# Two attentions rebuilt in head pairs, with bias, mask and minimum in one VectorE pass

## The chip, the cores and the metric

The kernel runs on one core of a Trainium2 chip. The metric is the device time of one execution in microseconds. Before the change it is 2356.97 us, the median of three runs (2353.76 to 2362.44). TensorE, VectorE, ScalarE, GpSimd and the DMA queues have their own instruction streams; they meet in semaphores that the kernel sets by hand.

## The reference, cut to what matters

Two transformer blocks on 256 tokens of width 2048, all in float32. The first block has 16 sliding-window heads with a distance bias and a sink ("swa") and 16 heads with a forget gate ("fox"). The second has 16 heads over 256 tokens and 256 context tokens, with a window mask and a sink.

```python
# block 1: swa heads, window 128, 2 key/value heads
s = jnp.einsum('bnqkgd,bnskd->bnkgqs', qb, kb) * scale
s = s - slopes[:, :, None, None] * dist
s = jnp.where(mask[None, :, None, None], s, -jnp.inf)
m = jnp.maximum(jnp.max(s, axis=-1, keepdims=True), sink)
p = jnp.exp(s - m)
p = p / (jnp.sum(p, axis=-1, keepdims=True) + jnp.exp(sink - m))
# block 1: fox heads, cT = cumsum of log f, per head
s = jnp.einsum('bqhd,bshd->bhqs', q_blk, k) * scale
s = s + c_blk[..., None] - cT[:, :, None, :]
s = jnp.where((q_pos[:, None] >= k_pos[None, :])[None, None], s, -jnp.inf)
p = jax.nn.softmax(s, axis=-1)
# block 2: windowed scores, context scores and a sink in one softmax
p = jax.nn.softmax(jnp.concatenate([s_win, s_ctx, s_sink], axis=-1), axis=-1)
# block 2 also needs silu(c) @ w_ada, in six parts of 2048 columns
m = jax.nn.silu(cond) @ w + b
```

Around the attentions stand large matrix products: in, out, up, down in the first block, in, out and an MLP in the second.

## The kernel before

**Large products.** A weight matrix comes in chunks of 512 columns. A chunk is 8 steps (6 in the last down part), a step 256 rows of the weight. For each step ScalarE rounds the weight to `w_hi` (`hi`, L526), VectorE makes the rest `w_lo` (`lo`, L811), and TensorE does 12 products of 512 columns (L1308 to L1310). `body` on each engine walks a chunk, three steps ahead of TensorE; four slots hold the split weights. The stages are in1, out1, up1a, down1a, up1b, down1b, up1c, down1c, in2, out2 and mlp2.

**The adaptive part.** GpSimd loads tiles of `w_ada` (L395), and VectorE adds each, times a column of silu, to an accumulator (`ada_op`, L826; L923 in in1), between its `lo` instructions. A part that serves tokens and context has two accumulators, so two VectorE instructions per tile. `ADA_ORDER` names the parts and their accumulators, `ADA_RUNS` cuts them into runs (part index, first tile, count). Run 1 (16 tiles, one accumulator) runs during attention 1, run 2 in out1, runs 3 to 6 in up1a, down1a, up1b and down1b; run 6 has two accumulators, up1c has none. After a part TensorE sums over partitions (`ada_sum`, L1353, 16 products of one column for each accumulator) and VectorE clears the accumulators (`ada_clear`, L848).

**Attention 1.** Heads 0 to 15 are swa, 16 to 31 fox. `qk1` holds the queries and keys turned, two heads in one tile of 128 rows: an even head has rows 0 to 63, an odd one rows 64 to 127. For one head `scores1` puts the bias into one of four PSUM banks of G by a product (L1413: `slope_id`, an identity times the head's slope made by ScalarE at L575, with the table of distances; for fox L1417 with `cT` and two mask products, L1419), then adds the score products of both query blocks (L1421: 128 and 256 columns, 64 rows deep). VectorE takes two maxima (L998, L999), scales and negates them (`shift`), ScalarE takes two exponentials out of PSUM with the row sums as accumulator output (L600, L602), TensorE turns the result (L1430), ScalarE copies it out of PSUM (L617), TensorE multiplies by the values (L1440 to L1443, 64 columns each), and every four heads VectorE divides (L985 to L987). All float32 products are two records each in the trace.

**Attention 2.** The same loop over 32 units of one head and one query block: scores of 512 columns (L1563), a mask product (L1565), maximum (L1206), exponential (L736), four transposes, copy (L749), four products by the values (L1577).

**What sets the order.** Each engine runs its list in program order. `attend` on TensorE issues three scores ahead, then for head n: scores of n+3, transposes of n, values of n-2.

## Time and profile before

| | |
|---|---|
| median of 3 runs | 2356.97 us |
| the profiled execution, its own time | 2354.01 us |
| its span, first to last instruction | 2352.3 us |
| TensorE busy | 96% of the span |
| VectorE busy | 65% |
| ScalarE busy | 46% |
| mean granted TensorE clock | 0.973 |

The profile is one execution. A row of a time line has the start in us from the start of the span, the duration, the engine and line, the operation, what it writes and reads, the shape, and how many instructions are merged (x4). Durations of TensorE records overlap, because their ends are modelled: how long a product holds the engine is read from start to start. A row with [idle before <-releaser] names what ended the engine's idle time.

### The profile page before, as it was taken

To read this page: it belongs to the slowest core of one execution; us is meant where nothing else is said; L and a number is where in the kernel's file an instruction comes from. 1 tells how busy PE (TensorE), PEld (TensorE's weight loads), DVE (VectorE), ACT (ScalarE), POOL (GpSimd) and SP (SyncE) were. 2 spreads that over 40 slices of the span, in tenths; PEclk is the share of its full clock that TensorE was granted. 3 is DMA by queue.
4 is the path that set the end of the run, shared out by engine and by line. 5 is a ranking of instruction groups with operands and counts; after the bars stand their busy time and mean duration, and the time that the engine had idled before them with its cause. 6 is when DMAs were issued, how large, how long until landed. Compare 5 with 4: busy or idle time off the path is not lost.

```text
span 2352.3 us, 30732 instructions
## 1 busy us (share of the span) xinstructions
PE 2251.9 (96%) x10407; PEld 1847.5 (79%) x10407; DVE 1538.2 (65%) x1750; ACT 1082.0 (46%) x1487; POOL 122.3 (5%) x217
## 2 busy tenths in 40 slices
PE   7999989899999999999997999898999999999997
PEld 5888678688888888788876776786888888888876
DVE  6886657778897888946665363455655655655555
ACT  5444554455534555335546344345444443443433
POOL 1000000100100000000000000001000000000000
PEclk9998999899999999989998999999999999999999
DMA  7886228678889787856554350155666666666752
GB/s 265 289 289 211 81 81 290 210 252 279 281 270 288 258 288 255 270 170 202 191 179 147 115 177 3 63 188 196 220 210 215 215 214 209 221 205 210 229 166 102
DMA packets 267279, 482.53 MB, mean 205 GB/s; under 512 B 15180, under 2 KB 107604, under 8 KB 265888
## 3 DMA queue, kind: packets, MB, share of 16 engines
q1 hardware_dynamic: 236544, 367.18, 47.1%
q0 software_dynamic: 29808, 113.63, 15.4%
q8 instruction: 81, 1.33, 0.2%
q10 hardware_dynamic: 816, 0.15, 0.0%
q14 instruction: 30, 0.25, 0.0%
HBM read 478.79 MB, written 2.11 MB: 204 GB/s over the span
## 4 chain that ended last, share of the span: by engine, by line
PE 94%; ACT 3%; DVE 2%; issue 1%; DMA 1%; ACTq 0%; SPq 0%; DVEq 0%
PE G L1308 27%; PE G L1310 27%; PE G L1309 27%; PE G L1563 1%; PE T L1353 1%; PE T L1477 1%; PE T L1430 1%; PE G L1421 1%; PE T L1577 1%; PE T L1342 1%; ACT junk L476 1%; PE G L1565 1%; PE G L1413 0%; PE G L1417 0%; DMA raw<-in_w_in 0%
## 5 line engine op out<-in xcount | busy, mean ns | idle before, releaser
L811 DVE TENSOR_TENSOR w_lo<-raw,w_hi 128x1024 fp32r<-128x1024 f32 x696 | 844.6, 1223 | 520.3 <-ACT w_hi L526 516.0
L526 ACT ACTIVATE w_hi<-raw 128x1024 fp32r<-128x1024 f32 x696 | 736.1, 1060 | 934.0 <-PE G L1310 932.5
L1308 PE MATMUL G<-w_hi,h_hi 128*128 128x512 f32 (+1 forms) x1920 | 755.3, 393 | 14.0 <-ACT w_hi L526 7.6
L1309 PE MATMUL G<-w_lo,h_hi 128*128 128x512 f32 (+1 forms) x1920 | 750.3, 391 | 0.0
L1310 PE MATMUL G<-w_hi,h_lo 128*128 128x512 f32 (+1 forms) x1920 | 749.9, 391 | 0.0
L1308 PEld LDWEIGHTS G<-w_hi,h_hi 128*128 128x128 f32 x1920 | 365.2, 190 | 89.8 <-ACT w_hi L526 8.6
L1310 PEld LDWEIGHTS G<-w_hi,h_lo 128*128 128x128 f32 x1920 | 364.7, 190 | 75.4
L1309 PEld LDWEIGHTS G<-w_lo,h_hi 128*128 128x128 f32 x1920 | 365.1, 190 | 73.5
L1308 PE MATMUL G<-w_hi,a_hi 128*128 128x512 f32 x896 | 352.6, 393 | 5.0 <-issue 2.9
L1310 PE MATMUL G<-w_hi,a_lo 128*128 128x512 f32 x896 | 349.9, 391 | 0.0
L1309 PE MATMUL G<-w_lo,a_hi 128*128 128x512 f32 x896 | 349.8, 390 | 0.0
L826 DVE SCALAR_TENSOR_TENSOR ada_acc<-ada_w,silu,ada_acc 128x1024 f32<-128x1024 f32 x160 | 204.9, 1280 | 61.4 <-DMA ada_w<-in_w_ada 60.8
L1308 PEld LDWEIGHTS G<-w_hi,a_hi 128*128 128x128 f32 x896 | 168.9, 189 | 44.1 <-issue 7.2
L1310 PEld LDWEIGHTS G<-w_hi,a_lo 128*128 128x128 f32 x896 | 168.9, 188 | 35.6
L1309 PEld LDWEIGHTS G<-w_lo,a_hi 128*128 128x128 f32 x896 | 169.1, 189 | 35.2 <-issue 0.5
L395 POOL DMA_DIRECT2D ada_w<-in_w_ada x192 | 101.7, 530 | 1417.8 <-DVE ada_acc L826 1082.0
L923 DVE SCALAR_TENSOR_TENSOR ada_acc<-ada_w,silu,ada_acc 128x1024 f32<-128x1024 f32 x64 | 79.2, 1279 | 0.0
L1068 DVE SCALAR_TENSOR_TENSOR conv<-T,convw,conv 128x255 f32<-128x255 f32 (+1 forms) x176 | 72.7, 475 | 9.4 <-ACT conv L659 7.0
L1206 DVE TENSOR_REDUCE mx<-G 128x1 f32<-128x512 f32 x32 | 22.1, 692 | 47.3 <-PE G L1565 47.3
L1342 PE MATMUL T<-ident,y 128*128 128x128 f32 x96 | 18.0, 358 | 32.0 <-ACT y L487 24.9
L1091 DVE TENSOR_TENSOR y<-y,G 128x512 f32<-128x512 f32 x56 | 35.9, 683 | 16.0 <-PE G L1310 16.0
L549 ACT ACTIVATE u_buf<-G,rstdx 128x512 f32<-128x512 f32 x44 | 27.9, 686 | 36.1 <-PE G L1310 36.1
(215 smaller groups left out, 1338.6 us busy)
## 6 DMA issues: line engine op xcount, KB each, us to landing
ada_w<-in_w_ada POOLq DMA_DIRECT2D x192, 512.0 KB, 4.9
raw<-in_w_up SPq DMA_DIRECT2D x176, 512.0 KB, 5.7
raw<-in_w_mlp_up SPq DMA_DIRECT2D x128, 512.0 KB, 4.6
raw<-in_w_mlp_down SPq DMA_DIRECT2D x128, 512.0 KB, 4.8
raw<-in_w_in SPq DMA_DIRECT2D x104, 512.0 KB, 5.2
raw<-in_w_down SPq DMA_DIRECT2D x88, 512.0 KB, 5.6
raw<-in_w_out SPq DMA_DIRECT2D x64, 512.0 KB, 5.0
raw<-in_w_in SPq DMA_DIRECT2D x8, 272.0 KB, 4.2
```

Of the source, the lines that this page charges most:

```text
L395: pool.dma_start(ada_tiles(run)[:, half, :], w_ada[:, bass.ds(t + first // 2, 1), part * D + half * ADA_HALF:part * D + (half + 1) * ADA_HALF]
L526: act.activation(w_hi[:, s % 4], raw[:, s // 2 % 4, STEPK * (s % 2):STEPK * (s % 2) + STEPK, :], ACT.Copy).then_inc(hi_ready, 1)
L549: act.activation(dst(b), G[:, 2 * parity + b, 0:width], func, scale=scale).then_inc(bank_evac, 1)
L811: dve.tensor_tensor(w_lo[:, s % 4], raw[:, s // 2 % 4, STEPK * (s % 2):STEPK * (s % 2) + STEPK, :], w_hi[:, s % 4].bitcast(F32), ALU.subtr ...
L826: ins = dve.scalar_tensor_tensor(out=acc[:, half, :], in0=ada_tiles(run)[:, half, :], scalar=silu[:, c, bass.ds(dt + (first + k) // 2, 1)] ...
L923: ins = dve.scalar_tensor_tensor(out=ada_acc[:, c, half, :], in0=ada_w[:, half, :], scalar=silu[:, c, bass.ds(i * 2 + k // 4, 1)], in1=ada ...
L1068: ins = dve.scalar_tensor_tensor(out=conv[:, j, k:TOK], in0=tt(0)[:, j, 0:TOK - k], scalar=convw[:, tap, bass.ds(t + dt, 1)], in1=conv[:, ...
L1091: dve.tensor_tensor(y[:, b, c * N:c * N + N], y[:, b, c * N:c * N + N], G[:, 2 * (c % 2) + b, :], ALU.add).then_inc(bank_evac, 1)
L1308: pe.matmul(out, ah, wh, start=f, stop=False)
L1309: pe.matmul(out, ah, wl, start=False, stop=False)
L1310: mm = pe.matmul(out, al, wh, start=False, stop=l)
L1342: mm = pe.transpose(tt(g % 2)[:, j, b * P:b * P + P], src[:, b, (4 * g + j) * P:(4 * g + j + 1) * P], ident[:])
```

## The change

It rebuilds both attentions and moves the adaptive part's runs.

- The bias of the swa heads no longer comes from a product. Queries are scaled by scale/slope as they are copied out of PSUM (`qscale`), and VectorE does one pass out of PSUM (`tensor_tensor_reduce`): score plus table, times minus the slope (or minus the scale), written to SBUF, with the minimum against the negated sink as accumulator output. In the fox heads and in attention 2 the masks are in this pass too; the fox heads keep one bias product of 384 columns, now in the rounded format of the large products (`select`, `cT`), for which `cT` is split into a rounded part and its rest, in rows 0 to 15 and 32 to 47.
- `exps1` and `exps2` read SBUF and have no accumulator output. The row sum comes from a column of ones beside the values (`vx1`, `vx2`, 65 columns), filled by GpSimd and ScalarE.
- The unit of the loops is a pair of heads. The scores of a pair go out one head at a time: both blocks of the even head, then both of the odd one. TensorE's order is: transposes of pair j, scores of pair j+2, values of pair j-1. In attention 1 ScalarE copies the turned even head and VectorE the odd one. VectorE divides after every pair.
- The slope copies (L575) are gone. No adaptive tile is taken during attention 1: out1 has run 1 with two accumulators, up1c gets 16 tiles with one accumulator, and down1b has one accumulator in place of two. The first tile of a run is written by a product alone, so the clears are gone. The sum that was in up1a is in down1a, the double sum moves from up1c to up1b, and down1c gets one.

```diff
-ADA_RUNS = ((0, 0, 32), (1, 0, 16), (1, 16, 16), (2, 0, 32), (4, 0, 16), (3, 0, 32), (4, 16, 16), (5, 0, 32))
+ADA_ORDER = ((0, (0, 1)), (3, (2,)), (1, (0, 1)), (4, (2,)), (2, (0,)), (5, (0,)))
...
+ADA_RUNS = ((0, 0, 32), (2, 0, 16), (1, 0, 32), (2, 16, 16), (3, 0, 32), (4, 0, 16), (4, 16, 16), (5, 0, 32))
...
+    t[:, C_QS:C_QS + 8] = SCALE / SLOPES[2 * np.arange(8)[None, :] + p // DH]
...
+    vx1 = place("vx1", [P, NB, 18, PV], "tmp")
...
-        for h in range(HEADS):
-            act.activation(slope_id[:, h, :], ident[:], ACT.Copy, scale=float(slopes[h] / SCALE)).then_inc(slope_ready, 1)
...
+            ins.then_inc(qk_act, 1)
+        act.wait_ge(v_ones, 1)
+        for b in range(NB):
+            ins = act.activation(vx1[:, b, 0:2, 0:DH], p1[:, b, VA:VA + 2 * DH].rearrange("p (h d) -> p h d", d=DH), ACT.Copy)
+        ins.then_inc(va_ready, 1)
+
+        def exps1(j):
+
+            for i in range(2):
+                n = 2 * j + i
+                act.wait_ge(masked, n + 1)
+                act.activation(sm1[:, n % 4, 0:P], sm1[:, n % 4, 0:P], ACT.Exp, scale=-1.0,
+                               bias=nm[:, j % 4, 2 * i:2 * i + 1])
+                act.activation(sm1[:, n % 4, P:3 * P], sm1[:, n % 4, P:3 * P], ACT.Exp, scale=-1.0,
+                               bias=nm[:, j % 4, 2 * i + 1:2 * i + 2]).then_inc(p_ready, 1)
+            if j < 8:
+                act.wait_ge(es_in, j + 1)
+                act.activation(es[:, j % 4, :], es[:, j % 4, :], ACT.Exp).then_inc(es_ready, 1)
...
+                if first + k < 2 and run != ADA_LAST:
+                    ins = dve.tensor_scalar(acc[:, half, :], ada_w[:, half, :], silu[:, c, 0:1], None, ALU.mult)
+                else:
+                    ins = dve.scalar_tensor_tensor(out=acc[:, half, :], in0=ada_tiles(run)[:, half, :],
+                                                   scalar=silu[:, c, bass.ds(dt + (first + k) // 2, 1)],
+                                                   in1=acc[:, half, :], op0=ALU.mult, op1=ALU.add)
             ins.then_inc(ada_used, 1)
...
 
...
+            else:
+                ins = dve.tensor_copy(qk1[:, 4 * g + 2:4 * g + 4, :], tt(g % 2)[:, 2:4, :])
+            ins.then_inc(qk_dve, 1)
...
+        for c0, n in ((0, P), (P, TOK)):
+            ins = dve.tensor_scalar(cT[0:48, c0:c0 + n], G[0:48, 1, 0:n], -1 / SCALE, None, ALU.mult)
+        link(ins)
+        for c0, n in ((0, P), (P, TOK)):
+            ins = dve.scalar_tensor_tensor(out=cT[32:48, c0:c0 + n], in0=G[32:48, 1, 0:n], scalar=-1 / SCALE,
+                                           in1=cT[32:48, c0:c0 + n].bitcast(F32), op0=ALU.mult, op1=ALU.subtract)
+        ins.then_inc(c_ready, 1)
         for g in range(2, 6):
             turned1(g)
...
-        def shift(n, slot, cols, nsinks):
...
+        def masks1(j):
+
+            dve.wait_ge(s_ready, j + 1)
+            for i in range(2):
+                n = 2 * j + i
+                if j >= 2:
+                    dve.wait_ge(pt_turned, n - 3)
+                table, scale, limit = ((ALI, -float(SLOPES[n]), nsink[:, 0, n:n + 1]) if n < HEADS else (CAU, -SCALE, BIG))
+                for k, (c0, w) in enumerate(((0, P), (P, 2 * P))):
+                    ins = dve.tensor_tensor_reduce(out=sm1[:, n % 4, c0:c0 + w], in0=G[:, n % 4, c0:c0 + w],
+                                                   in1=tab1[:, table + c0:table + c0 + w], scale=scale, scalar=limit,
+                                                   op0=ALU.add, op1=ALU.min,
+                                                   accum_out=nm[:, j % 4, 2 * i + k:2 * i + k + 1])
+                ins.then_inc(masked, 1)
             if exped is not None:
                 dve.wait_ge(es_ready, exped)
-                link(dve.tensor_tensor(r, r, es[:, b % 4, :], ALU.add))
-            link(dve.reciprocal(r, r))
-            dve.tensor_tensor(dst.rearrange("p k (h d) -> p k h d", d=DH),
-                              T[:, 2 + b % 2, :].rearrange("p (k h d) -> p k h d", k=NB, d=DH),
...
+            dve.tensor_tensor(dst.rearrange("p k (i d) -> p k i d", d=DH),
...
+        for j in range(HEADS):
+            dve.wait_ge(pt_turned, 2 * j + 2)
+            if j >= 2:
+                dve.wait_ge(pt_used, 2 * j - 2)
+            dve.tensor_copy(pt1[:, (2 * j + 1) % 4, :], T[:, 1, 0:3 * P]).then_inc(pt_dve, 1)
+            if j + 2 < HEADS:
+                masks1(j + 2)
+            if j >= 1:
+                outputs1(j - 1)
...
                 if k % 2:
-                    ada_op(2, 4 * c + k // 2)
...
-        for g, n, run_up, run_down, fin_up, fin_down in (("a", 8, 3, 4, None, 2), ("b", 8, 5, 6, None, 3),
-                                                         ("c", 6, None, None, 4, None)):
+        for g, n, run_up, run_down, fin_up, fin_down in (("a", 8, 2, 3, None, 1), ("b", 8, 4, 5, 2, 3),
+                                                         ("c", 6, 6, None, None, 4)):
...
+            first, each = (4, 4) if n == 8 else (1, 3)
+            body(s0, adas=[(run_up, k) for k in range(first)])
...
-        def scores1(n):
-
...
-            if n >= 4:
-                pe.wait_ge(p_ready, n - 3)
-            if n < HEADS:
-                pe.matmul(bank[:, 0:3 * P], slope_id[:, h, :], tab1[:, ALI:ALI + 3 * P], start=True, stop=False)
-            else:
-
-
-                pe.matmul(bank[:, 0:3 * P], ident[:, h:h + 1].broadcast_to([P, P]), cT[:], start=True, stop=False)
-                for c0 in (0, 2 * P):
-                    pe.matmul(bank[:, c0:c0 + P], ident[:], tab1[:, CAU:CAU + P], start=False, stop=False)
-            for blk, (c0, w) in enumerate(((0, P), (P, 2 * P))):
-                mm = pe.matmul(bank[:, c0:c0 + w], qk1[rows, q, P * blk:P * blk + P], qk1[rows, k, 0:w],
-                               start=False, stop=blk == NB - 1)
+        def scores1(j):
+
+            if j >= 2:
+                pe.wait_ge(masked, 2 * j - 2)
+            if j >= 8:
+                for n in (2 * j, 2 * j + 1):
+                    h = n - HEADS
+                    pe.matmul(G[:, n % 4, 0:3 * P], select[:, h:h + 1].broadcast_to([P, P]), cT[:], start=True, stop=False)
+            for i in range(2):
+                for blk, (c0, w) in enumerate(((0, P), (P, 2 * P))):
+                    n = 2 * j + i
+                    h = n % HEADS
+                    q, k = (h // 2, 8 + h // 8) if n < HEADS else (10 + h // 2, 18 + h // 2)
+                    rows = slice(DH * i, DH * i + DH)
+                    mm = pe.matmul(G[:, n % 4, c0:c0 + w], qk1[rows, q, P * blk:P * blk + P], qk1[rows, k, 0:w],
+                                   start=j < 8, stop=j < 8 or blk == NB - 1)
             mm.then_inc(s_ready, 1)
...
+                v = n // 8 if n < HEADS else 2 + n - HEADS
+                out = T[:, 2 + j % 2, 2 * PV * i:2 * PV * i + 2 * PV]
+                pe.matmul(out[:, 0:PV], pt1[:, n % 4, 0:P], vx1[:, 0, v, :], start=True, stop=True)
+                pe.matmul(out[:, PV:2 * PV], pt1[:, n % 4, P:2 * P], vx1[:, 0, v, :], start=True, stop=False)
+                pe.matmul(out[:, PV:2 * PV], pt1[:, n % 4, 2 * P:3 * P], vx1[:, 1, v, :],
+                          start=False, stop=True).then_inc(pt_used, 1)
...
+            scores(0)
+            scores(1)
+            for j in range(HEADS):
+                turn(j)
+                if j + 2 < HEADS:
+                    scores(j + 2)
+                if j >= 1:
+                    pv(j - 1)
+            pv(HEADS - 1)
...
-                ada_sum(1)
...
+        def scores2(j):
+            t, blk = j // 2, j % 2
+            if j >= 2:
+                pe.wait_ge(masked, 32 + 2 * j - 2)
+            if j == 1:
```

`masks2`, `exps2`, `pv2` and `turn2` are built as in attention 1, with 512 columns for a head and block.

How the order of instructions changes. First TensorE in the swa heads of attention 1, in a steady stretch, before (one head):

```order
L1413 MATMUL G<-tab_74,slope_id 128x384
L1421 MATMUL G<-qk_73 128x128
L1421 MATMUL G<-qk_73 128x256
L1430 MATMUL T<-ident,sm_69 128x128 x3
L1440 MATMUL T<-p_68,pt_70 128x64
L1441 MATMUL T<-p_68,pt_70 128x64
L1443 MATMUL T<-p_68,pt_70 128x64
```

and now, TensorE at the same place (two heads; `vx_71` are the values with their ones):

```order
L1478 MATMUL T<-consts,sm_69 128x128 x6
L1471 MATMUL G<-qk_73 128x128
L1471 MATMUL G<-qk_73 128x256
L1471 MATMUL G<-qk_73 128x128
L1471 MATMUL G<-qk_73 128x256
L1501 MATMUL T<-vx_71,pt_70 128x65
L1502 MATMUL T<-vx_71,pt_70 128x65
```

The bias product of each head is gone, and the four score products of a pair stand together; four more value products follow the last row.

VectorE in the same stretch, before (two heads, with one adaptive tile):

```order
L998 TENSOR_REDUCE mx<-G 128x1
L999 TENSOR_REDUCE mx<-G 128x1
L971 TENSOR_SCALAR nm<-mx,nsink 128x2
L998 TENSOR_REDUCE mx<-G 128x1
L999 TENSOR_REDUCE mx<-G 128x1
L971 TENSOR_SCALAR nm<-mx,nsink 128x2
L976 TENSOR_TENSOR es<-nm,sink_110 128x8
L826 SCALAR_TENSOR_TENSOR ada_acc<-ada_w,silu,ada_acc 128x1024
```

and now, VectorE for one pair (ISA is the fused pass, the row with nm alone the reading of its accumulator):

```order
L1048 COPY pt_70<-T 128x384
L1031 ISA sm_69,nm<-G,tab_74,nsink 128x128
L1031 ISA nm 128x1
L1031 ISA sm_69,nm<-G,tab_74,nsink 128x256
L1031 ISA nm 128x1
L1031 ISA sm_69,nm<-G,tab_74,nsink 128x128
L1031 ISA nm 128x1
L1031 ISA sm_69,nm<-G,tab_74,nsink 128x256
L1031 ISA nm 128x1
L1002 TENSOR_TENSOR es<-nm,sink_111 128x4
L1013 TENSOR_TENSOR rs<-T,es 128x4
L1014 RECIPROCAL rs<-rs 128x4
```

Maxima and adaptive tile make room for the fused passes, a copy and a division for each pair (its product, 128x2x128, follows the last row).

VectorE in the second chunk of down1b, before, and then now:

```order
L848 MEMSET ada_acc 128x2048
L811 TENSOR_TENSOR w_lo<-raw,w_hi 128x1024
L826 SCALAR_TENSOR_TENSOR ada_acc<-ada_w,silu,ada_acc 128x1024
L826 SCALAR_TENSOR_TENSOR ada_third<-ada_w,silu,ada_third 128x1024
L811 TENSOR_TENSOR w_lo<-raw,w_hi 128x1024
```

Here it is in the changed kernel, VectorE again:

```order
L870 MEMSET ones_again 128x1
L837 TENSOR_TENSOR w_lo<-raw,w_hi 128x1024
L855 SCALAR_TENSOR_TENSOR ada_acc<-ada_w,silu,ada_acc 128x1024
L837 TENSOR_TENSOR w_lo<-raw,w_hi 128x1024
L855 SCALAR_TENSOR_TENSOR ada_acc<-ada_w,silu,ada_acc 128x1024
```

Between two `w_lo` stands one adaptive instruction in place of two, and the clear is gone.

## Rows read from the trace of the kernel before

**Rows 1.** The page: busy us (share of the span) and instructions by engine.

```profile
PE 2251.9 (96%) x10407; PEld 1847.5 (79%) x10407; DVE 1538.2 (65%) x1750; ACT 1082.0 (46%) x1487; POOL 122.3 (5%) x217
```

**Rows 2.** Windows (swa heads, in2, attention 2): us, busy PE, PEld, DVE, ACT, POOL; clock.

```profile
242.00:278.00 36.00, 36.00 (x188) 22.45 (x188) 26.83 (x62) 19.75 (x75) 3.69 (x7) 1.00 0.31 90
...
1330.00:1350.00 20.00, 20.00 (x90) 16.57 (x89) 3.68 (x3) 4.14 (x4) 0.00 (x0) 1.00 0.32 98
1403.00:1491.00 88.00, 88.00 (x513) 61.28 (x514) 32.83 (x77) 44.94 (x103) 1.42 (x2) 1.00 0.09 32
```

**Rows 3.** Time line of TensorE: one swa head, bias to bias.

```profile
256.20 0.86 PE L1413 MATMUL G<-tab,slope_id 128*128 128x384 f32 x2
256.99 0.92 PE L1421 MATMUL G<-qk 64*128 64x128 f32 x4
257.84 0.55 PE L1430 MATMUL T<-ident,sm 128*128 128x128 f32 x3
258.23 0.33 PE L1440 MATMUL T<-p,pt 128*128 128x64 f32 x2
...
258.84 0.54 PE L1413 MATMUL G<-tab,slope_id 128*128 128x384 f32 x1
```

**Rows 4.** Time line of TensorE: bias and masks of one fox head.

```profile
292.36 0.86 PE L1417 MATMUL G<-cT,ident 128*128 128x384 f32 x2
293.06 0.61 PE L1419 MATMUL G<-tab,ident 128*128 128x128 f32 x4
293.60 0.37 PE L1421 MATMUL G<-qk 64*128 64x128 f32 x1
```

**Rows 5.** Time line of TensorE: one unit of attention 2.

```profile
1438.57 1.12 PE L1563 MATMUL G<-k2t,q2t 64*128 64x512 f32 x2
1439.62 0.49 PE L1565 MATMUL G<-tab,ident 128*128 128x128 f32 x2
1439.94 0.60 PE L1430 MATMUL T<-ident,sm 128*128 128x128 f32 x4
1440.38 0.56 PE L1577 MATMUL T<-p,pt 128*128 128x64 f32 x4
...
1441.32 0.69 PE L1563 MATMUL G<-k2t,q2t 64*128 64x512 f32 x1
```

**Rows 6.** Time line of VectorE, then of ScalarE, in the swa heads.

```profile
257.95 0.29 DVE L998 TENSOR_REDUCE mx<-G 128x1 f32<-128x128 f32 x1 [1.76 <-PE G L1421]
258.15 0.41 DVE L999 TENSOR_REDUCE mx<-G 128x1 f32<-128x256 f32 x1
...
258.43 0.49 ACT L617 ACTIVATE pt<-T 128x384 f32<-128x384 f32 x1 [1.29 <-PE T L1430]
258.87 0.37 ACT L600 ACTIVATE sm<-G,nm 128x128 f32<-128x128 f32 x1
259.13 0.19 ACT L600 ACTIVATION_READ_ACCUMULATOR sm<-G,nm 128x1 f32 x1
```

**Rows 7.** Time line of ScalarE: the slope copies at the end of in1.

```profile
204.96 3.30 ACT L575 ACTIVATE slope_id<-ident 128x128 f32<-128x128 f32 x16
```

**Rows 8.** TensorE's waits, 200 to 215 us: total, times, longest.

```profile
PE G L1308 <- ACT w_hi L526: 2.4, 1, 2.4
```

**Rows 9.** Time line of VectorE before attention 1: the making of cT.

```profile
236.81 0.38 DVE L957 MEMSET cT<- 128x384 f32 x1 [0.27 <-PE G L1389]
...
237.43 0.40 DVE L959 TENSOR_SCALAR cT<-G 16x256 f32<-16x256 f32 x1
```

**Rows 10.** Time line of VectorE, second chunk of down1b: two neighbouring w_lo.

```profile
951.83 1.22 DVE L811 TENSOR_TENSOR w_lo<-raw,w_hi 128x1024 fp32r<-128x1024 f32 x1
...
955.36 1.22 DVE L811 TENSOR_TENSOR w_lo<-raw,w_hi 128x1024 fp32r<-128x1024 f32 x1
```

**Rows 11.** TensorE's waits, 915 to 1020 us (down1b).

```profile
PE G L1308 <- issue: 2.1, 4, 0.6
PE G L1308 <- ACT w_hi L526: 1.6, 2, 1.2
```

381 lines of the change are left out of this document (188 added, 193 removed).

## The prediction

> **What bounds the kernel now.** I read the page's busy table first: TensorE is busy for 96% of the span, VectorE for 65%, ScalarE for 46% [rows 1]. Then the windows of the two attentions: in the swa heads and in attention 2 TensorE is busy without a break at a granted clock of 1.00, while VectorE is busy for 75% and 37% and ScalarE for 55% and 51% [rows 2]. So both attentions last as long as TensorE's list, and what leaves that list is gained, as long as nobody else becomes the last. The third view is TensorE's own time line, read from start to start [rows 3 to 5]; it gives the prices. The fourth is TensorE's waits in the stages whose side work moves [rows 8, 11].
>
> **Attention 1, TensorE.** A swa head takes 258.84 - 256.20 = 2.64 us: bias 0.79, scores 0.85, transposes 0.39, values 0.61 [rows 3]. A fox head has the same parts, but its bias takes 0.70, because no product of another height follows it, and its masks 0.54 [rows 4]: 2.64 - 0.09 + 0.54 = 3.09. Sixteen of each make 91.7 us. The 0.09 is a wait as TensorE goes over to products 64 rows deep. In the score products themselves there is more of this kind: the bias sends 384 columns through twice in 0.70, and the scores, which are the same 384 columns twice, need 0.85.
>
> A swa pair then costs: 0.09 for going over, 0.85 for the first head's scores, at most 0.70 for the second's (the bias row, same columns, no change of height between them; 0.64 if its first weight load is hidden), 2 x 0.39 for the transposes, 2 x 0.61 for the values. That is 3.64; with the lower prices 3.5; I take 3.6, where two heads took 5.29. The 65th column is no new instruction, and the value products are paced by something other than their columns (0.61 for six records of 64, 0.39 for three of 128), so it costs nothing. A fox pair adds two products of 384 columns in the rounded format. Steady in2 has 88 to 90 such products of 512 columns in 20 us, 0.227 each [rows 2]; 384 columns are 0.17 by columns and 0.227 at most. With 0.17 a fox pair takes 3.95 against 6.18. Eight pairs of each: 28.8 + 31.6 = 60.4.
>
> The start is new: no value products fill it. Scores of pair 0 take 1.6, VectorE's pass over its two heads about 1.7, two exponentials each 0.4 to 0.5, and ScalarE has the exponentials of pair 1 in front of the copy of pair 0, which pair 1's transposes wait for. Laid out by hand, TensorE idles some 0.5 before the transposes of pair 0's second head and 1.0 before those of pair 1: +1.5 (0 to 3). **Attention 1: 91.7 to 61.9, -29.8.**
>
> **Does VectorE follow?** Its list for a swa pair: four fused passes, four accumulator reads, one copy of 384 columns, the sink's addition, and add, reciprocal and product of the division. The trace before has no fused pass. Its nearest rows are the maxima out of PSUM, 0.29 for 128 and 0.41 for 256 columns, the second starting 0.20 after the first [rows 6]. The nearest row for an accumulator read is ScalarE's, 0.19 [rows 6]. Low end: passes 0.20 + 0.33 and reads of 0.06 each, 1.3 a pair; high end: 0.29 + 0.41 and reads of 0.19, 2.2. I take 1.8, nearer to neither, because starts overlap in those rows but the reads must wait for the pass. The copy is about 0.5 (ScalarE's of the same size 0.49 [rows 6]), the sink 0.2, the division about 0.85 with its two links. Sum 3.35, from 2.85 to 3.75, against TensorE's 3.6. In fox pairs sink and addition are gone: 2.9 against 3.95. ScalarE: four exponentials of 0.37 to 0.47, a copy of 0.49, a sink of 0.2, 2.4 in all; the accumulator reads are off its list. The chain from the scores of a pair to its transposes two pairs later is scores 1.6, passes 1.8, last exponentials 0.9, transposes 0.8 and some 0.3 of signals, 5.4 for two pairs, against 7.2. So TensorE stays last, with VectorE close behind.
>
> **Attention 2.** A unit takes 2.75: scores 1.05, mask 0.32, transposes 0.44, values 0.94 with the going over [rows 5]. A pair after the change: 0.10, 1.05, 0.85 for the second head (1.05 less the weight load at its start and the wait at its end, 0.1 each), 2 x 0.44, 2 x 0.90: 4.7 against 5.49. Start 0.6. VectorE needs about 1.8 for two passes of 512, ScalarE 2.7; both have room. 32 x 2.75 = 88.0 becomes 75.8, **-12.2** (-11 to -13). ScalarE's four copies of values and GpSimd's fill before it stand in in2, where `w_hi` is three steps ahead: nothing, or 1 if that lead is used up.
>
> **Around attention 1.** The slope copies hold ScalarE for 3.30 [rows 7], and TensorE waits 2.4 for the `w_hi` behind them [rows 8]: **-2.4**. Before the scores VectorE gets more to do: `cT` had a clear of 0.38 and two scalings of up to 0.40 [rows 9]; two more passes of that kind, one for `select`, one more subtraction, and each of the first two copies of queries in halves. That is about 1.6, of which 0.5 fits in VectorE's waits; the rest delays the copies that the scores wait for: **+1.1** (0 to 2). The last division is of 256 columns in place of 512: -0.3. GpSimd's fill and copies of values lie between its last in1 tile and out1's row, where it only waits.
>
> **The adaptive part.** VectorE pays 3.53 for a `w_lo` and two adaptive instructions [rows 10], so 1.17 and two of 1.18; TensorE's step is 12 x 0.227 = 2.72. In down1b four steps running have two of them, and TensorE waited 2.1 + 1.6 = 3.7 [rows 11]; the clear goes too. With one accumulator a step costs VectorE 2.35 and nothing is late: **-5** (-3.7 to -7, the smaller pauses included). Out1 takes over the two accumulators, but alternates them with `w_lo`: 8 x 1.17 + 8 x 1.18 + two evictions of 0.68 is 20.2 a chunk against 21.8 for TensorE. It fits, and the last eviction may come later: **+0.5** (0 to 3). Up1b gets the double sum while VectorE also has four tiles a chunk: **+1** (0 to 3). Up1c has room for three. The sums themselves are as many as before: 0.
>
> **Sum.** -29.8 - 12.2 - 2.4 + 1.1 - 0.3 - 5 + 0.5 + 1 = -47.1. The profiled execution took 2354.0, so 2306.9. The median of the runs lies 3.0 above that execution, within their spread of 8.7; I leave it there: 2307.
>
> **Rivals.**
>
> *The two heads' scores overlap.* The even head uses rows 0 to 63, the odd one 64 to 127, in different banks, and now they follow each other directly. No row shows two such neighbours, so neither for nor against, but the waits at the change of height speak for a separate mode. One head at a time, only the last pass of the even head and the first of the odd one can meet: 0.43 a pair in attention 2 (a pass of 512, half of 0.85), 0.21 in attention 1. 16 x 0.64 = 10.2: 2297. The Trainium skill, "TensorE: Matmul & The Clock Gate", Part 3 on row and column tiling, says that matmuls in different row groups run concurrently, starting some 4 ns apart. By that rule the time is this rival's, without it the forecast's; no run here shows it yet.
>
> *VectorE becomes the last in the swa pairs.* At its high end, 3.75 to 3.9, it adds 8 x 0.3 = 2.4. If the fused pass takes twice as long per column, 768 columns add 0.8 a pair: 4.4 for swa, level with fox: 8 x 0.8 = +6, with late first pairs up to +10: 2313 to 2317. The rows speak against doubling, as two-input passes of 1024 columns take 1.2 [rows 10]. The Trainium skill, "Vector Engine (DVE) Microarchitecture Reference", section 7, warns that such an operation with two SBUF sources of full width runs at half throughput for want of a port for the accumulator. Here one source is in PSUM, and the pass of 1024 columns with two SBUF sources, in 1.22 [rows 10], is not halved; taken for the fused pass, the warning would give this rival's time.
>
> *The adaptive work bites where it went.* If out1, up1b and down1a each wait as down1b did (3.7 to 7), +15: 2322. For it: out1's margin is 1.6 a chunk. Against: its tiles are spread, not four in a row.
>
> *Slower than before.* The fused pass is an instruction that no row shows. Were it slow per column, VectorE would set both attentions. At c us per column, 16 pairs of 768 and 16 of 1024 columns, plus about 50 for the rest of its list, reach 180 us and the 5 gained elsewhere at c = 0.0048. From 4.8 ns per column the kernel is slower than before; at 6 ns by 35 us, 2389. Every VectorE row here is near 1.2 ns. That the rebuilding changes nothing would need VectorE at exactly that point.
>
> **Chances.** Forecast 0.43; overlap 0.28; VectorE last 0.14; adaptive work 0.10; slower 0.02; within 0.5% 0.03. The range goes from the overlap with the lower prices of a pair (2297 less 8) to the adaptive rival: 2289 to 2322. About 0.5%, 12 us, is what a measurement can tell from no change. Faster 0.95, same 0.03, slower 0.02.
>
> **What would show it.** In the time line of TensorE: a swa pair of 3.6 and a fox pair of 3.95, from one group of six transposes to the next, and a unit pair of 4.7 in attention 2; with overlap 3.4, 3.75 and 4.3, and two score products of different heads starting almost together. No wait of TensorE for VectorE or ScalarE inside the attentions after pair 1. Fused passes of 0.3 and 0.45 with reads of 0.06 to 0.19. VectorE busy for some 90% of the swa stretch. No ScalarE wait at the end of in1, no waits in down1b, and out1 at 21.8 a chunk. The prediction is wrong if TensorE waits in every pair, if the granted clock in the attentions falls from 1.00 to its lower level (1.2 GHz), or if out1 or up1b grow by more than 3 each.

## The result and the profile after

The changed kernel takes 2284.29 us (median of 4 runs, 2280.0 to 2287.6), the kernel before beside it 2356.76 us. The ratio is 0.9689, 95% interval 0.9676 to 0.9701: faster by 72.5 us. The prediction said faster, with 2307 us in a range from 2289 to 2322: the sign was right, the time lies 5 us below the range. The profiled execution of the changed kernel took 2284.72 us against 2354.01, 69.3 us less where 47.1 were forecast.

The busy line of its page stands where [rows 1] stood:

```profile
PE 2182.4 (96%) x10231; PEld 1807.9 (79%) x10231; DVE 1526.3 (67%) x1841; ACT 1066.9 (47%) x1375; POOL 125.7 (6%) x220
```

The shares hardly moved. The windows of the two attentions (swa pairs, fox pairs, attention 2), which answer to [rows 2], have the granted clock at 1.00 throughout. TensorE is idle for 1.7 of the first 20 us and for 1.1 of the 63, both at the start of an attention; behind it (244 to 290 and 1366 to 1421 us) the view of its waits is empty:

```profile
core 0: us, PE busy (x) PEld busy (x) DVE busy (x) ACT busy (x) POOL busy (x), PEclk, DMA share, GB/s
238.00:258.00 20.00, 18.29 (x158) 14.54 (x158) 17.58 (x86) 14.97 (x45) 0.00 (x0) 1.00 0.01 1
258.00:290.00 32.00, 32.00 (x274) 27.35 (x273) 22.69 (x105) 21.15 (x59) 0.00 (x0) 1.00 0.01 2
1358.00:1421.00 63.00, 61.89 (x449) 46.95 (x450) 29.44 (x93) 42.20 (x75) 1.42 (x2) 1.00 0.12 44
```

So after its first pairs each attention is still as long as TensorE's list, and the list must be shorter than I made it. Its time line over a swa pair and the next transposes answers to [rows 3] (start, duration, engine, line, operation, shape, how many merged):

```profile
249.30 0.83 PE L1478 MATMUL T<-consts,sm 128*128 128x128 f32 x6
250.06 0.93 PE L1471 MATMUL G<-qk 64*128 64x128 f32 x8
250.92 0.44 PE L1501 MATMUL T<-vx,pt 128*128 128x65 f32 x2
251.19 0.39 PE L1502 MATMUL T<-vx,pt 128*128 128x65 f32 x2
251.42 0.39 PE L1503 MATMUL T<-vx,pt 128*128 128x65 f32 x2
251.64 0.39 PE L1501 MATMUL T<-vx,pt 128*128 128x65 f32 x2
251.86 0.39 PE L1502 MATMUL T<-vx,pt 128*128 128x65 f32 x2
252.09 0.39 PE L1503 MATMUL T<-vx,pt 128*128 128x65 f32 x2
252.31 0.50 PE L1478 MATMUL T<-consts,sm 128*128 128x128 f32 x3
```

From 249.30 to 252.31 a pair takes 3.01 us, not 3.6. Transposes take 0.76 (priced 0.78) and values 1.39 (priced 1.22: each product now takes 0.22 or more, also the one that took 0.16 with 64 columns). The scores are far off: eight records, both heads, start at 250.06 and what follows starts at 250.92, 0.86 us, the 0.85 of one head's four records in [rows 3]. Attention 2 shows the same, against [rows 5]:

```profile
1379.22 0.93 PE L1478 MATMUL T<-consts,sm 128*128 128x128 f32 x7
1380.08 1.13 PE L1626 MATMUL G<-k2t,q2t 64*128 64x512 f32 x4
1381.13 2.00 PE L1646 MATMUL T<-vx,pt 128*128 128x65 f32 x16
```

Two heads' scores of 512 columns in 1.05 us, which is what one head takes. Taken singly, the eight records of the swa pair start at 250.059, .073, .274, .286, .385, .398, .604 and .616: in couples, 12 to 14 ns apart, the first couple with 128 columns each, as the second, the last two with 256. In attention 2 they are 7 ns apart. The program has 128, 128, 256 and 256 columns of the even head first and the same of the odd head after them, so the starts do not follow the program. A record does not name its head; that a couple is the same pass of both heads is the reading that fits, and the experiments test it.

Where the 69.3 us lie, from the two traces (TensorE's first and last record of each stretch, the bias products of the kernel before counted with the scores; the third column is a second profile of the same changed kernel, from the experiments, and its change stands in brackets):

| stretch | before | after | again | change, forecast |
|---|---|---|---|---|
| start to first score of attention 1 | 241.8 | 237.9 | 238.5 | -3.9 (-3.3), -1.3 |
| attention 1 | 92.3 | 52.7 | 52.7 | -39.5, -29.8 |
| from there to the first score of attention 2 | 1068.8 | 1067.2 | 1069.8 | -1.5 (+1.1), -3.8 |
| attention 2, to its last value product | 88.1 | 63.2 | 63.2 | -24.9, -12.2 |
| the rest | 861.3 | 861.9 | 859.8 | +0.6 (-1.5), 0 |

The two attentions alone are 22.4 us better than forecast, which is the whole error. The stretch between the attentions takes 1063.9 to 1073.1 us in eight profiles with the same work there, and the last stretch 859.7 to 863.0, so single stages in them are read with care.

### The profile page after: what moved, and what is told of

The parts are those of the page before. It is cut to its first block, busy times and chain, and to the rows that moved or that the text cites. A ratio compares the mean times of both kernels' runs of the same rounds, so it can differ in the third digit from the quotient of the medians.

```text
span 2283.0 us, 30329 instructions
## 1 busy us (share of the span) xinstructions
PE 2182.4 (96%) x10231; PEld 1807.9 (79%) x10231; DVE 1526.3 (67%) x1841; ACT 1066.9 (47%) x1375; POOL 125.7 (6%) x220
## 4 chain that ended last, share of the span: by engine, by line
PE 93%; ACT 3%; DVE 2%; DMA 1%; issue 1%; ACTq 0%; SPq 0%; DVEq 0%; POOLq 0%; POOL 0%
PE G L1362 28%; PE G L1364 28%; PE G L1363 28%; PE T L1407 1%; PE T L1537 1%; PE T L1646 1%; PE T L1396 1%; PE T L1478 1%; ACT junk L491 1%; PE G L1626 1%; DMA x<-in_x 1%; PE G L1471 1%; PE T L1501 0%; DMA raw<-in_w_in 0%; PE T L1451 0%
## 5 line engine op out<-in xcount | busy, mean ns | idle before, releaser
L1364 PEld LDWEIGHTS G<-w_hi,h_lo 128*128 128x128 f32 x1920 | 363.3, 189 | 75.3
L855 DVE SCALAR_TENSOR_TENSOR ada_acc<-ada_w,silu,ada_acc 128x1024 f32<-128x1024 f32 x122 | 153.6, 1279 | 31.7 <-DMA ada_w<-in_w_ada 31.7
L855 DVE SCALAR_TENSOR_TENSOR ada_third<-ada_w,silu,ada_third 128x1024 f32<-128x1024 f32 x60 | 76.9, 1281 | 56.3 <-DMA ada_w<-in_w_ada 56.3
L945 DVE SCALAR_TENSOR_TENSOR ada_acc<-ada_w,silu,ada_acc 128x1024 f32<-128x1024 f32 x64 | 79.2, 1279 | 0.0
L1396 PE MATMUL T<-consts,y 128*128 128x128 f32 x96 | 19.1, 374 | 31.0 <-ACT y L502 24.2
```

What stands on the lines that cost most here:

```text
L855: ins = dve.scalar_tensor_tensor(out=acc[:, half, :], in0=ada_tiles(run)[:, half, :], scalar=silu[:, c, bass.ds(dt + (first + k) // 2, 1)] ...
L945: ins = dve.scalar_tensor_tensor(out=ada_acc[:, c, half, :], in0=ada_w[:, half, :], scalar=silu[:, c, bass.ds(i * 2 + k // 4, 1)], in1=ada ...
L1364: mm = pe.matmul(out, al, wh, start=False, stop=l)
L1396: mm = pe.transpose(tt(g % 2)[:, j, b * P:b * P + P], src[:, b, (4 * g + j) * P:(4 * g + j + 1) * P], ident)
```

## The experiments

The theory after the result: **the products of the two heads use different halves of TensorE's rows and run side by side from the first pass to the last, whatever their order in the program; the forecast's only large error is the price of the second head's scores.** The rivals were that the order matters, and that the pair is short for another reason: VectorE, or a cheaper change of height (going between products 128 and 64 rows deep).

**Both heads on the same rows.** Nothing but the rows of the operands changes, in both attentions.

```diff
-                    rows = slice(DH * i, DH * i + DH)
+                    rows = slice(0, DH)
```

> The changed kernel with the score products of both heads of a pair on partitions 0 to 63, in both attentions: the odd head's scores are worked out from the even head's rows of the queries and keys, so the odd heads' outputs are those of other scores; number, size and order of all instructions stay. Theory 'the whole error of the forecast is the second head's scores, which ran beside the first's': its price comes back, 16 x 0.59 in attention 1 (swa pair 3.01 to 3.60, fox pair 3.36 to 3.95) and 16 x 0.83 in attention 2 (unit pair 3.87 to 4.70), 22.7 us in all: 2307 us (2302 to 2310), which is what the forecast gave. Rival 'the pair is short for another reason, such as cheaper passes between row groups, and VectorE sets 3.01 in the swa pairs': under 8 us more, 2292 us or less.

Measured: 2304.0 us, ratio to before 0.977 (0.9749 to 0.9791), 20 us more than the changed kernel. Its time line of TensorE:

```profile
249.76 1.03 PE L1471 MATMUL G<-qk 64*128 64x256 f32 x5
250.72 0.44 PE L1501 MATMUL T<-vx,pt 128*128 128x65 f32 x2
...
252.11 0.82 PE L1478 MATMUL T<-consts,sm 128*128 128x128 f32 x6
252.87 1.57 PE L1471 MATMUL G<-qk 64*128 64x128 f32 x8
254.37 0.32 PE L1501 MATMUL T<-vx,pt 128*128 128x65 f32 x1
```

The same eight records now take 254.37 - 252.87 = 1.50 us. The swa pair is 3.65, the fox pair 4.00, the unit pair (one pair of heads in attention 2, 3.87 in the changed kernel) 4.72; attention 1 takes 61.7 us and attention 2 75.3. The forecast had 3.6, 3.95, 4.7, 61.9 and 75.8. This is the kernel that I had predicted, and the rival with at most 8 us more is out.

**Alternate order.** In attention 1 the loop over blocks goes outside, the one over heads inside.

```diff
-            for i in range(2):
-                for blk, (c0, w) in enumerate(((0, P), (P, 2 * P))):
+            for blk, (c0, w) in enumerate(((0, P), (P, 2 * P))):
+                for i in range(2):
```

> The changed kernel with attention 1's score products of a pair issued alternately (first block of the even head, first block of the odd head, second block of the even, second of the odd) and not one head at a time. Theory 'the halves run free': the changed kernel's trace shows the eight records of a pair in couples 0.012 to 0.014 us apart although the even head's products all stand first, so order does not matter; 2284 us (2281 to 2287), swa pair 3.01 us, fox pair 3.36, starts in couples as before. Rival 'only neighbours overlap' (the forecast's rival A): alternate order would overlap more than one head at a time; the pair would shorten by up to 0.4 us, 16 times, 2278 us or less.

Measured: 2286.41 us, 0.9705 (0.9686 to 0.9724); pairs of 3.00, 3.35 and 3.87 us, attention 1 52.6 us. The scores of a swa pair take 0.86 us as before:

```profile
250.02 0.93 PE L1471 MATMUL G<-qk 64*128 64x128 f32 x8
250.88 0.44 PE L1501 MATMUL T<-vx,pt 128*128 128x65 f32 x2
```

The couples are now 6 to 7 ns apart in place of 12 to 14, and that is all that the order changes: 0.01 us a pair. "Only neighbours overlap", the limit that I had set in the rival of the overlap, falls.

**A product of all rows between the heads.**

```diff
             for i in range(2):
+                if i and j < 8:
+                    pe.matmul(G[:, (2 * j + 1) % 4, 384:392], ident, ident[:, 0:8], start=True, stop=True)
...
+                if i:
+                    pe.matmul(G[:, (2 * j + 1) % 4, 0:8], ident, ident[:, 0:8], start=True, stop=True)
```

> The changed kernel with one more small product (128 rows, 8 columns) between the even and the odd head's scores, in the 8 swa pairs of attention 1 and the 16 units of attention 2; no result is changed. Theory 'the halves run free of each other only as long as no product that uses all 128 rows stands between them': the overlap is gone there, and the small product comes on top (0.2 to 0.4 us each): swa pair 3.01 to between 3.7 and 4.0, unit pair 3.87 to between 4.8 and 5.1, fox pair 3.36 as before: 2284 + 8 x 0.85 + 16 x 1.1 = 2309 us (2303 to 2315). Rival 'overlap in the records is an artefact and the scores' cost is small for another reason': only the small products are paid, 24 x 0.2 = 5 us, 2289 us.

Measured: 2316.18 us, 0.9824 (0.9808 to 0.9841). TensorE in a swa pair:

```profile
249.81 0.83 PE L1480 MATMUL T<-consts,sm 128*128 128x128 f32 x6
250.57 0.92 PE L1473 MATMUL G<-qk 64*128 64x128 f32 x4
251.42 0.39 PE L1467 MATMUL G<-consts 128*128 128x8 f32 x2
251.74 0.92 PE L1473 MATMUL G<-qk 64*128 64x128 f32 x4
252.59 0.44 PE L1503 MATMUL T<-vx,pt 128*128 128x65 f32 x2
```

A product of 8 columns costs its own 0.32 us (251.42 to 251.74) and parts the heads: 0.85 for each. The swa pair goes to 4.16, a little above the expected 3.7 to 4.0, the unit pair to 5.23, also above; the fox pair, without the product, stays at 3.36. The attentions account for 7.4 + 19.8 = 27.2 of the 32 us; the rest is in the large products between them, where no edit was made, and I have no cause for it beyond their spread.

**The adaptive plan alone**, in the kernel before: its `ADA_ORDER` and `ADA_RUNS`, first tiles by a product, no clears, nothing in attention 1, sums as in the changed kernel.

```diff
-ADA_ORDER = ((0, (0, 1)), (2, (0,)), (3, (0,)), (4, (0,)), (1, (1, 2)), (5, (0,)))
+ADA_ORDER = ((0, (0, 1)), (3, (2,)), (1, (0, 1)), (4, (2,)), (2, (0,)), (5, (0,)))
...
-            if n % 2:
-                ada_op(1, n // 2)
```

> The kernel before, with the changed kernel's plan of the adaptive matrices alone (order of the sums, runs per stage, first tiles multiplied instead of cleared and added, none in attention 1, two accumulators in out1), attentions as before. By the stages of the changed kernel's trace: out1 +4.0, up1a -4.7, down1a +2.0, up1b and up1c 0 together, down1b -6.8, down1c +5.3: -0.2 us, 2356.5 us (2353 to 2359), so the rebuilt attentions and what stands between carry all of the gain. Rival, the forecast's terms for these steps (down1b -5, out1 +0.5, up1b +1, about -3.5, the sum in up1a moved at no net cost): 2353 us, and then out1's +4.0 has another cause than the adaptive work.

Measured: 2351.13 us, median of 10 runs, 0.9973 (0.996 to 0.9986): 3.3 to 9.4 us less than before. My expectation, read off one pair of profiles, had 2356.5 (-0.2) and missed; the forecast's -3.5 is inside the interval. Attention 1 is 92.26 us in both, to the hundredth: VectorE's adaptive tiles there had cost nothing. Of the profiled difference of 5.5 us 2.7 lie ahead of attention 1, where this edit changes nothing; the clock there, shown with the slope copies below, differs between the two profiles. One pair of profiles says no more about the gain than the interval of the runs.

**The slope copies back.**

```diff
+        for h in range(HEADS):
+            act.activation(ada_third[:].rearrange("p a n -> p (a n)")[:, P * h:P * h + P], ident, ACT.Copy, scale=1.0).then_inc(qk_junk, 1)
         body(s0 + 64)
```

> The changed kernel with 16 copies of 128x128 on ScalarE put back ahead of in1's last 8 tiles, where the kernel before made its slope matrices (they write an unused place). Theory: they hold ScalarE's w_hi back by 3.3 us, TensorE waits 2.4 us, in1's last chunk goes from 21.24 to about 24.4 us: +3 us, 2287 us (2286 to 2289). Rival 'ScalarE has that much slack now': the last chunk stays at 21.2 us and nothing is paid, 2284 us; the earlier start of attention 1 would then come from the clock in in1's tail alone.

> The changed kernel once more, so that the three small edits beside it have it on the same chip: 2284 us (2281 to 2287). By the theory that out1's last chunk of 46.7 us in the first profile of it was chance (44.8 in three variants that leave out1 alone, 44.3 in the kernel before), that chunk is 44.8 us here.

Measured, on one chip: 2287.57 us (0.9695, 0.9676 to 0.9714) with the copies, 2283.24 us (0.9671, 0.9651 to 0.969) without. TensorE's waits over the tail of in1 show the old wait, as in [rows 8]:

```profile
PE G L1365 <- ACT w_hi L542: 2.4, 1, 2.4
```

In the profiles 2.0 us arrive at the first score (240.47 against 238.52). The windows of the tail say what the copies cost and what they seem to give back, first with the copies, then without:

```profile
211.20:214.60 3.40, 3.40 (x17) 3.40 (x16) 3.16 (x4) 1.72 (x2) 0.00 (x0) 0.50 0.83 269
219.90:224.80 4.90, 4.90 (x47) 4.90 (x45) 1.28 (x3) 2.67 (x5) 2.55 (x3) 1.00 1.00 338
224.80:229.00 4.20, 4.20 (x21) 4.20 (x21) 0.00 (x0) 0.00 (x0) 0.00 (x0) 0.50 0.22 87
```

```profile
209.00:216.00 7.00, 7.00 (x60) 7.00 (x59) 5.96 (x6) 4.86 (x6) 0.00 (x0) 1.00 0.95 308
219.00:226.80 7.80, 7.80 (x39) 7.80 (x38) 0.00 (x0) 0.00 (x0) 0.60 (x1) 0.50 0.48 187
```

With the copies the clock is at 0.50 for 3.4 us soon after the wait; the kernel before has the same at 212.1. Without the wait it stays at 1.00. From the last product of 512 columns to the adaptive sum, TensorE takes 12.65 us in all ten profiles without the copies, 16.8 in this one and in that of the kernel before, and 15.3 in the adaptive plan alone, which has the copies and the wait but no low clock behind it. So the copies cost 2.6 us there, and 4.1 when the clock falls after the wait.

The adaptive sum behind it is 64 products of one column, and the clock falls a second time within it, in every profile: 2.4 us after its first product in the changed kernel (215.4 and 217.8), 4.9 with the copies (219.9 and 224.8). TensorE was busy without a pause until then; before the sum it ran products of 272 columns and a few transposes at 1.00. A one-column product takes 0.213 us at 0.50 and 0.11 at 1.00, so the sum lasts 8.9 us in the profile with the copies and 10.7 in the one beside it (11.2 in the first of the changed kernel, 11.3 before): 1.8 us by chance for the copies. The removal is worth 2.0 us in this pair of profiles and 4.3 in the medians, whose intervals overlap; the forecast had 2.4, the wait alone.

The second run also speaks on out1's last chunk: 45.8 us in this profile, where 44.8 was expected, 44.8 in three variants, 46.7 in the first, 44.3 before. It varies.

**More work for VectorE in attention 1**: the 256-column pass of each head twice.

```diff
+                ins = dve.tensor_tensor_reduce(out=ada_w[:, 0, 256 * (n % 4):256 * (n % 4) + w], in0=G[:, n % 4, c0:c0 + w],
+                                               in1=tab1[:, table + c0:table + c0 + w], scale=scale, scalar=limit,
+                                               op0=ALU.add, op1=ALU.min,
+                                               accum_out=nmx[:, n % 4:n % 4 + 1])
```

> The changed kernel with the 128x256 pass of every head in attention 1 made twice (the second to an unused place): 2 x (0.48 + 0.08) less the overlap of neighbours, some 1.0 us more for VectorE in each pair. VectorE is busy 17.58 of 20 us in swa pairs (2.65 of 3.01) and 22.69 of 32 in the later pairs (2.39 of 3.36). Theory 'TensorE sets the pairs, VectorE has the slack that its idle time shows': swa pair 3.65 us, fox pair 3.4, +0.64 x 8 + 0.05 x 8 = +5.5 us, 2290 us (2288 to 2292). Rival (the forecast's second rival, VectorE in a closed round with TensorE and ScalarE already at 3.01): every added us is paid, swa pair 4.0, fox pair up to 4.3: +8 to +15 us, 2292 to 2299 us.

Measured: 2289.28 us, 0.9706 (0.9674 to 0.9738), 5 to 6 us more. VectorE's time line (its pair runs from one copy to the next, 3.57 us, without idle time):

```profile
253.68 0.55 DVE L1053 COPY pt<-T 128x384 f32<-128x384 f32 x1
254.15 0.34 DVE L1032 CUSTOM_DVE_ANT_0 sm<-G,tab,nsink 128x128 f32<-128x128 f32 x1
254.41 0.08 DVE L1032 DVE_READ_ACCUMULATOR2_ANT nm<- 128x1 f32 x1
254.41 0.48 DVE L1032 CUSTOM_DVE_ANT_0 sm<-G,tab,nsink 128x256 f32<-128x256 f32 x1
254.82 0.08 DVE L1032 DVE_READ_ACCUMULATOR2_ANT nm<- 128x1 f32 x1
254.82 0.48 DVE L1036 CUSTOM_DVE_ANT_0 ada_w<-G,tab,nsink 128x256 f32<-128x256 f32 x1
255.22 0.08 DVE L1036 DVE_READ_ACCUMULATOR2_ANT nmx<- 128x1 f32 x1
255.22 0.35 DVE L1032 CUSTOM_DVE_ANT_0 sm<-G,tab,nsink 128x128 f32<-128x128 f32 x1
...
257.25 0.55 DVE L1053 COPY pt<-T 128x384 f32<-128x384 f32 x1
```

The added pass takes 0.40 us from start to start, so 0.80 a pair; the list without it is 3.57 - 0.80 = 2.77 us against TensorE's 3.01. VectorE has a slack of 0.24 us in a swa pair, no more. The rival, a closed round in which every added microsecond is paid, would have given 3.81 at this price, and doesn't exist. The fox pairs are back at 3.36 after two longer ones at the change from swa (4.33 and 3.40).

**A bias product back** ahead of each swa head's scores.

```diff
+            if j < 8:
+                for n in (2 * j, 2 * j + 1):
+                    pe.matmul(G[:, n % 4, 0:3 * P], ident, tab1[:, CAU:CAU + 3 * P], start=True, stop=False)
```

> The changed kernel with a product of 128 rows and 384 columns, two passes, ahead of each swa head's scores (identity times the causal mask, added once more, which alters no probability), where the kernel before had its bias product. Theory 'TensorE sets the pairs': each costs what the row of the kernel before shows, 0.79 to 0.85 us, 16 times: swa pair 3.01 to 4.6 or 4.7, fox pair 3.36 as before: +13 us, 2298 us (2296 to 2300). Rival 'VectorE sets the swa pairs' : half of it or less is paid, 2291 us or less.

Measured: 2292.25 us, 0.9723 (0.9699 to 0.9747), 8 to 9 us more. In the steady pairs every added microsecond is paid, so TensorE is last; but the product costs less than expected, and the total, short of the expected 2296 to 2300, alone would not decide against the rival's 2291:

```profile
250.88 1.46 PE L1463 MATMUL G<-tab,consts 128*128 128x384 f32 x4
252.27 0.93 PE L1474 MATMUL G<-qk 64*128 64x128 f32 x8
```

Two take 252.27 - 250.88 = 1.39 us with the 0.09 for going over to 64 rows, and the pair grows from 3.01 to 4.30: 0.64 each, where the row of before had 0.79 in every head. Sixteen of them are 10.3 us; the first pairs, where TensorE had idle time, hide the rest of it. Before, each head went over and back once; a pair does it once, with or without the bias.

**Towards a faster kernel.** Three edits around out1 and the preparations (the two transposed copies of an activation, rounded and rest, that each stage begins with).

```diff
+            elif mid is not None:
+                tile(0, 0, n - 1)
+                tile(0, 1, n)
+                mid()
...
-                if k % 2:
-                    ada_op(1, 4 * c + k // 2)
+                if 8 * c + k in OUT1_AT:
+                    ada_op(1, OUT1_AT.index(8 * c + k))
...
+                if 1 <= t <= n:
+                    scale(t - 1)
+                if pre and t == 2 and n > 3:
+                    pre(3)
+                if t >= 2:
+                    rest(t - 2)
```

`mid` issues x's reload; `OUT1_AT` is 1, 3, 4, 6, 8, 10, 12, 13, 15, 17, 19, 20, 22, 24, 26, 27.

> The changed kernel with three edits around out1: the reload of x is issued after the first two adaptive tiles of out1 instead of after all sixteen (it landed at 398.2 us, 1.9 us after the residual could begin); out1's adaptive work ends three w_lo earlier, so that the last two evictions do not stand behind it (2.0 us late in the profiled execution); and in VectorE's part of each preparation the last group's residual or scaling is put before the first group's h_lo, which waits 2.4 us for ScalarE. Theory 'the chain between out1 and up1 is VectorE's order': up to 2.0 + 1.9 + 3 us there and about 1 us in each of the other preparations: 2277 us (2273 to 2281). Rival 'ScalarE's squares and h_hi set the preparations': 1 to 3 us, 2282 us.

> The changed kernel with the two edits in out1 alone: x's reload after the first two adaptive tiles, and the adaptive work ending three w_lo earlier. Theory 'the last evictions and the reload stand behind the adaptive work': out1's last chunk 44.8 to 42.9 us or less, 2282 us (2280 to 2284). Rival 'all of the gain of the three edits comes from the order in the preparations': 2284 us, as the changed kernel.

> The changed kernel with one edit: in VectorE's part of each preparation the last group's residual or scaling stands before the first group's h_lo. Theory 'each preparation ends 1 to 3 us earlier': 2279 us (2276 to 2282), the last chunks of out1 and down1c and the chunks that hold the two preparations of in2 shorter by that. Rival 'ScalarE's squares and h_hi set the preparations': 2283 us or more.

Measured: all three 2276.14 us, 0.9651 (0.9629 to 0.9673). The two in out1 alone 2286.13 us, 0.9687 (0.9668 to 0.9706), nothing against 2283.24 on the same chip. The order in the preparations alone 2277.39 us, 0.965 (0.9631 to 0.9669), 5.8 us less than the changed kernel beside it. VectorE after out1, first in the changed kernel (its second profile), then with the edit:

```profile
403.57 0.87 DVE L904 TENSOR_SCALAR conv<-T,gains 128x256 f32<-128x256 f32 x2
406.87 1.23 DVE L913 TENSOR_TENSOR h_lo<-u_buf,h_hi 128x1024 fp32r<-128x1024 f32 x1 [2.43 <-ACT h_hi L531]
408.01 1.41 DVE L1080 SCALAR_TENSOR_TENSOR x<-y,rstd,x 128x512 f32<-128x512 f32 x2
```

```profile
400.47 0.88 DVE L904 TENSOR_SCALAR conv<-T,gains 128x256 f32<-128x256 f32 x2
401.26 1.40 DVE L1091 SCALAR_TENSOR_TENSOR x<-y,rstd,x 128x512 f32<-128x512 f32 x2
403.80 1.23 DVE L913 TENSOR_TENSOR h_lo<-u_buf,h_hi 128x1024 fp32r<-128x1024 f32 x1 [1.13 <-ACT h_hi L531]
```

Before the edit VectorE idles 2.43 us for `h_hi` with the last residual ready behind it, for which TensorE's last transposes wait. With it that residual runs at 401.26, inside the wait, of which 1.13 us are left. From out1's first `w_hi` to that of up1a it is 103.7 us against 110.3, and 107.7 to 111.2 in the profiles that leave out1 and this order alone. Part of that is the clock: from 395 to 425 us its mean is 0.89 against 0.77. With the version of all three edits, level with it, it is the fastest of the study. Its difference to the changed kernel, 0.965 against 0.9671, is within the two intervals; the runs themselves (2274.2 to 2278.1 against 2278.8 to 2285.8, five each) don't overlap.

## Why the prediction was wrong, point by point

- **The view and the bound were right.** Attentions as long as TensorE's list, clock 1.00, VectorE close behind in swa pairs, no wait inside after the first pairs. VectorE's margin (2.77 of 3.01 us; estimated 3.35 of 3.6) came out right by luck: its list and TensorE's were both taken 0.6 too long.
- **The step that failed: "at most 0.70 for the second's" in the swa and fox pair, and 0.85 for the second head in attention 2.** Both are 0.01 or less. With the same rows for both heads they are 0.64 and 0.85, and the pairs are 3.65, 4.00 and 4.72 us, attentions 61.7 and 75.3 us, against 61.9 and 75.8 forecast. The term is mis-sized by 9.0 + 12.1 = 21.1 us between these two kernels (attention 1 61.7 against 52.7, attention 2 75.3 against 63.2).
- **Why I took it.** The first rival named the overlap and was given 0.28, but cut to one pass a pair (10.2 us, 2297) by an assumption that no row bore: that a product waits in the program's order for the one before it, even on other rows. The couples in an order that is not the program's, and the alternate order at 2286 us, show that a product on one half does not wait for those ahead of it on the other. The rival with the forecast's full prices, 16 x (0.70 + 0.85) = 24.8 us, would have given 2282. The Trainium skill, "TensorE: Matmul & The Clock Gate", Part 3, says that products in different row groups run concurrently some 4 ns apart: they do run together here, but 6 to 14 ns apart. The same part calls products strictly first in, first out; taken over the whole engine, that was my limit, and here it doesn't hold between the halves. I should have let the range reach to the full overlap: 8 us below 2282, it would have ended near 2274.
- **Start of attention 1**: +1.5 forecast. From the first score to the second group of transposes it takes 2.64 + 2.71 us, with 0.96 us idle before the first group and 0.61 before the second; the next pair takes 3.06, and then the steady 3.01 begins. Right in kind and size. Attention 1 with the same rows is 61.7 against 61.9.
- **The parts of a pair.** 3.65 against 3.6 is in part luck. With the same rows, transposes and going over are 0.76 (priced 0.87), scores 1.50 (1.55), values 1.39 (1.22): the values cost 0.17 more than forecast, the rest less.
- **Bias**: its row had 0.79, its product alone is worth 0.64. The sum was unaffected, since I had built the pair from the parts that stay and not by subtraction.
- **Fused pass**: 0.35 and 0.48 us for 128 and 256 columns, reads 0.08, 0.75 for 512 columns; forecast 0.3, 0.45 and 0.06 to 0.19. The rivals with VectorE last and with the slow pass are out. The price of the first has a slip: a pass at half speed adds 0.8 to VectorE's 3.35, which gives 4.15 us for a swa pair, and not to TensorE's 3.6 (4.4). The Trainium skill, "Vector Engine (DVE) Microarchitecture Reference", section 7, warns of half throughput with two SBUF sources, which no fused pass here has. With one source in PSUM the pass grows from 0.35 to 0.75 us between 128 and 512 columns, 1.04 ns a column, where `w_lo`, two sources in SBUF, takes 1.22 us for 1024, 1.2 ns a column: it is not halved.

```profile
L1031 DVE CUSTOM_DVE_ANT_0 sm<-G,tab,nsink 128x256 f32<-128x256 f32 x12 | 5.8, 480 | 0.0
L1031 DVE CUSTOM_DVE_ANT_0 sm<-G,tab,nsink 128x128 f32<-128x128 f32 x12 | 4.2, 348 | 1.0 <-PE G L1471 1.0
L1250 DVE CUSTOM_DVE_ANT_0 sm<-G,tab,nsink 128x512 f32<-128x512 f32 x22 | 15.6, 749 | 18.0 <-PE G L1626 18.0
```

- **Around attention 1**: -2.4 for the copies and +1.1 for `cT` gave -1.3; the stretch moved by -3.9 and -3.3 in two profiles. The copies' term had the wait and left out the 3.4 us of low clock behind it: up to the sum it is 4.1. From the last product of the sum to attention 1 it is 10.5 us before, 11.3 and 11.7 after, +0.8 and +1.3, near the +1.1, though the clock is not the same there; no run tests the +1.1 apart.
- **The adaptive part**: -5, +0.5 and +1 forecast; alone it gives -3.3 to -9.4. down1b's waits of [rows 11] are gone, as forecast: TensorE has no wait there, and from its first large product to that of up1c it takes 99.0 us before, 91.9 and 92.8 after. Out1, from its first `w_hi` to that of up1a, grew from 107.2 us to 111.2 and 110.3 in the two profiles, more than the 3 that I had named as a sign of being wrong; but in the variants that leave it alone it is 107.7 to 109.3, so +0.5 to +4 against +0.5. Its first chunk holds 1.4 to 1.6 of the growth in the two profiles, and that is the clock, not the adaptive work: it is at 0.50 from 303.2 and 304.3 us for 3.4 us, as out1's products begin, while in the variant with the copies it is at 1.00 by then and the chunk takes 21.9, as before. Up1b grew by 12 to 14 us and up1c shrank by 13.6, since the double sum changed places. Moving the adaptive tiles away from its last evictions brought 108.6 and no time in the end. The rival of +15 is out. Between the attentions the changed kernel's profiles show -1.5 and +1.1, less than the plan alone gives; I can't say where the difference lies, since the same work varies there by 9 us.

## What to carry to other kernels

When a change puts float32 products of 64 rows on different row halves and in different banks next to each other, price the second at nothing, as it cost here, or at least let the range hold that case, also when the program issues all of one before the other; keep products of all rows out from between them, for even 8 columns cost 0.3 us and the overlap. A pair built from the prices of its parts by start to start came out close (3.65 against 3.6, 4.72 against 4.7), with parts 0.1 to 0.2 off that cancelled; the large doubt belonged to concurrency. A wait that is taken away can give back more than itself: behind the 2.4 us here stood 3.4 us of low clock. And where an engine waits for a partner at a hand-over (`h_hi` here), look for the step behind the wait that could stand ahead of it: that one change of order was worth 5.8 us, nearly as much as the whole adaptive plan (6.6 in the medians).

## What the runs showed of the hardware

- Two float32 products of 64 rows, on rows 0 to 63 and 64 to 127, into different PSUM banks, start 6 to 14 ns apart and take the time of one (0.86 us for 384 columns twice, 1.05 for 512 twice), in both orders of issue that were run.
- On the same rows the second head's products cost 0.64 and 0.85 us. The first costs 0.85 and 1.05: 0.2 us more, paid once for the run of such products. Products of 128 rows behind transposes of 128 rows, the same 384 columns twice, cost 0.64, so the 0.2 go with the change of height.
- A product of 128 rows and 8 columns between products of 64 rows takes 0.32 us and ends the overlap: 1.15 us for a swa pair, 1.36 for a unit pair.
- The granted clock fell to 0.50 within the sum of 64 one-column products in all thirteen profiles, 2.2 to 4.9 us after its first product, though TensorE's busy share was full (219.0 to 226.8: 7.80 of 7.80 us busy, clock 0.50). One such product takes 0.11 us at 1.00 and 0.213 at 0.50.
- A wait of 2.4 us at a clock of 1.00 was followed by 3.4 us at 0.50 in two profiles (211.2 to 214.6, 212.1 to 215.5) and by none in a third.
